# Products of the identity with itself ahead of 31 waits of TensorE, in a two-layer hybrid trunk kernel

## The chip, the cores and the metric

The kernel runs on one core of one Trainium2 chip. The metric is the device time of one execution in microseconds (us), the median of several executions. TensorE (PE in the rows) has a clock that the chip grants at one of two levels, 2.4 GHz (1.00 in the rows) and 1.2 GHz (0.50).

## What is computed

The reference is two layers of a hybrid backbone, for 128 context tokens and 256 latent tokens (384 in all, three tiles of 128) with 1024 channels, in float32. Cut to what matters here:

```
def trunk_layer(x, mod, p, ffn, is_moe, grid_pos, ctx_k, ctx_v, s0):
    shift1, scale1, gate1, shift2, scale2, gate2 = jnp.split(mod, N_MOD, axis=-1)
    h = rmsnorm(x, p['norms'][0]) * (1.0 + scale1) + shift1
    z = h @ p['w_in']
    ...
    o_a = block_attention(qa, k_all, v_all)
    o_b = chunk_gmlp(jax.nn.gelu(ub), jax.nn.gelu(vb), p['gmlp_norm'], p['gmlp_ws'], p['gmlp_bs'])
    o_c, s_fin = deltanet_mixer(qkvc, bc, ac, zc, p['dn_conv'], p['dn_a_log'], p['dn_dt_bias'], p['dn_norm'], s0)
    merged = g_a * (o_a @ wb[0]) + g_b * (o_b @ wb[1]) + g_c * (o_c @ wb[2])
    x = x + gate1 * rmsnorm(merged @ p['w_out'], p['norms'][1])
    h2 = rmsnorm(x, p['norms'][2]) * (1.0 + scale2) + shift2
    f = moe_swiglu(h2, *ffn) if is_moe else swiglu(h2, *ffn)
    x = x + gate2 * rmsnorm(f, p['norms'][3])
    return x, ka, va, s_fin

mod = (jax.nn.silu(c) @ ada_w[l] + ada_b[l])[:, None, :]
```

Layer 0 has the dense channel mixer, layer 1 the one with eight experts. The modulation vector `mod` is a product of its own, with 24 weight units of 2 MB each (12 a layer).

## The kernel before, in words

Each engine has its own program, and the engines meet through semaphores. TensorE's program is one long list that is executed strictly in its written order: a wait stops everything behind it on that engine. Weights come in units of up to 2 MB into a ring of four slots, loaded by SyncE's queue as soon as the last reader of a slot has let it go. ScalarE (ACT) rounds a unit to a high half, VectorE (DVE) or GpSimd (POOL) makes the low half, and TensorE forms each product three times (high with high, high with low, low with high). These long products (L1169 to L1171, L1205 to L1207, L1573 to L1575, L1595 to L1597, L1645 to L1647, L1707 to L1710) are most of the program.

Between them are short pieces in which TensorE takes turns with the other engines. In the order of a layer:

- `turn_x(layer, idx)` (L1142) multiplies the tokens with a diagonal of their norms, 3 token tiles by 8 channel blocks (L1152). At block 0 it waits per token tile for the diagonal of VectorE (`x_dg`), from block 4 on for the banks to be read (`h_a`, `h_d`).
- `ada_quads` and `ada_turn` (L1137, L1130) make the modulation. Their weight units (`in_ada_w`) share the ring; `ada_turn` waits for a copy by ScalarE (`ada_ev`).
- `feature_tile` (L1175): the first projections. Tile 1 waits for the low half of its weights (`p_lo`).
- The turn to attention and gating (L1295 to L1326): transposes of q and k (L1104, the line of all transposes through `tr`) after `a_ok`, then the gating products (L1319) after `tr_ev` and `v_ok`.
- Attention (L1372 to L1381): twelve steps, each with `scores` (L1341), `flip` (transposes, L1104, which wait for the exponentials, `at_e`) and `weigh` (L1362). `turn_o` transposes the outcome of a token tile after `at_n`.
- DeltaNet (from L1415): three rounds, whose gaps are filled with gate projections by `fill` (L1169 to L1171). It starts after `at_o`, and in its first round there is an `ada_turn`.
- The branch products, the output product (from L1554) with `gain_row` (L1158) ahead, then `turn_x(layer, 1)` and the channel mixer.
- At the end of layer 0 the units `n4` of the modulation (L1853) after `xk`, and then layer 1 begins with `turn_x(1, 0)`.

A product of two float32 operands is executed as two matmul instructions, so 12 such products are 24 in the trace. The order view counts products, the trace instructions.

Of the kernel before, what the change touches and what calls it, by code (L numbers as in the profile page):

```python
# [28 lines left out]
P = 128  # L29
# [5 lines left out]
NT = TOK // P  # L35
# [66 lines left out]
ADA_FIRST = (0, 1, 2, 3)  # L102
# [79 lines left out]
def build(nc, cst_d, x_prompt, x_sample, cache_k, cache_v, state_in, c, c_ctx, ada_w, ada_b, norms, w_in, qk_norm,  # L182
# [3 lines left out]
    with ctx:  # L186
# [913 lines left out]
        def _(pe):  # L1100
# [35 lines left out]

            def ada_quads(units, b):  # L1137
                for n in units:
                    for half in range(2):
                        ada_quad(n, half, b)  # L1140

            def turn_x(layer, idx, between=None, ks=range(KT)):  # L1142

                for k in ks:
                    if k == 4 and between:
                        between()
                    if k >= 4:
                        wait(pe, "h_d" if k % 2 else "h_a", layer, 4 * idx + (k - 4) // 2 + 1)
                    for t in range(NT):
                        if k == 0:  # L1150
                            wait(pe, "x_dg", layer, NT * idx + t + 1)
                        last = mm(B[T_BANK[k % 4]][:, t * P:(t + 1) * P], xt[:, t, k * P:(k + 1) * P], diag[:, t], start=True, stop=True)  # L1152
                    last.then_inc(S["xt_p"], 1)
# [21 lines left out]
            def feature_tile(layer, n):  # L1175

                bank_free(layer, n)
                wait(pe, "p_lo" if n else "v_lo", layer, lo_n(n // 4, n % 4) + 1)
                for k in range(KT):
# [35 lines left out]
            for layer in range(DEPTH):  # L1215
# [5 lines left out]
                if layer == 0:  # L1221
                    pe.wait_ge(sc_ok, 1)
                    turn_x(layer, 0, ks=range(4))
                    ada_quads(ADA_FIRST, 0)
                    ada_turn(ADA_FIRST, 0, KK_)
                    turn_x(layer, 0, ks=range(4, KT))
                    pe.wait_ge(ada_cp, set_end(ADA_FIRST))
                else:
                    turn_x(layer, 0, lambda: ada_turn(ADA_AT[0]["n4"], 7, ada_buf))

# [53 lines left out]
                for i, j0 in ((0, 8), (1, 4)):  # L1284
                    for t in range(NT):
# [7 lines left out]
                        last.then_inc(S["kvt_mm"], 1)  # L1293

                wait(pe, "a_ok", layer, 1)  # L1295
                pe.wait_ge(cache_in, 48 * (layer + 1))
# [16 lines left out]
                last.then_inc(S["tr_mm"], 1)  # L1313

                wait(pe, "tr_ev", layer, 6)
                wait(pe, "v_ok", layer, 1)
# [26 lines left out]

                def flip(i):
                    wait(pe, "at_e", layer, i + 1)
                    if i:
# [18 lines left out]

                def turn_o(t):
                    wait(pe, "at_n", layer, t + 1)
                    for j in range(4):
# [44 lines left out]

                eye2 = [eyeP.unsqueeze(1).to_broadcast([P, DNH, CHUNK])] * 2
                wait(pe, "at_o", layer, 3)  # L1415
                for pair in range(3):
# [22 lines left out]
                    if dn_ada:  # L1439
                        ada_turn(dn_ada, 0, dn_rows)  # L1440
                        pe.wait_ge(ada_cp, set_end(dn_ada))
                    fill(pair, "in")
# [86 lines left out]
                for m in range(8):  # L1529
# [8 lines left out]
                    for b in range(3):  # L1538
# [14 lines left out]
                        last.then_inc(S["br_mm"], 1)  # L1553
                ada_quads(at["wo"], 0)  # L1554
                pe.wait_ge(mod_ok, 4 * layer + 2)
                wait(pe, "br_ev", layer, 7)
                for half in range(2):
                    gain_row(layer, 2, 0, half, 2 + half)
                ada_turn(at["wo"], 0, ada_buf)
                wait(pe, "o_lo", layer, O_LO.index("me7") + 1)  # L1560
# [291 lines left out]

                if at["n4"]:  # L1853
                    wait(pe, "xk", layer, NT + 2)
                    ada_quads(at["n4"], 7)
# [1188 lines left out]
```

## Time and profile before

| | |
|---|---|
| median of 3 runs | 1894.83 us (1892.13 to 1901.94) |
| the profiled execution | 1898.18 us |
| its span, first to last instruction | 1896.4 us |
| mean granted clock over the span | 0.968 |
| TensorE busy | 1784.5 us, 94% |
| VectorE busy | 1001.0 us, 53% |
| ScalarE busy | 784.3 us, 41% |
| GpSimd busy | 257.8 us, 14% |

The profile is of one execution, 1.8 us longer than its span and 3.35 us above the median. A row of the timeline gives the start, the length, the engine and line, what is written and read, the number of instructions, and in brackets the idle time of that engine ahead of them and what ended it. A row of the windows view gives the busy time of each engine in a stretch and the clock granted in it.

### The profile page before, as it was taken

What the parts mean: (1) busy time and instruction counts of PE and PEld (TensorE: products, weight loads), DVE (VectorE), ACT (ScalarE), POOL (GpSimd) and SP (SyncE); (2) the same over time, 40 slices, a digit from 0 to 9 for tenths busy, and PEclk for the clock granted to TensorE, in tenths of its full rate; (3) what the DMA queues carried; (4) which work ended last, traced back from release to release, by engine and by line L of the source; (5) the groups of instructions that cost most, each with busy time, mean ns of one, the idle gap of its engine ahead of it and who ended that gap; (6) DMA issues with size and microseconds to landing.
All of it is one profiled execution on the core that took longest, in us unless ns stands there. A gap on an engine that the chain in (4) does not pass through costs nothing.

```text
span 1896.4 us, 31868 instructions
## 1 busy us (share of the span) xinstructions
PE 1784.5 (94%) x13834; PEld 1498.3 (79%) x13834; DVE 1001.0 (53%) x1288; ACT 784.3 (41%) x1090; POOL 257.8 (14%) x222
## 2 busy tenths in 40 slices
PE   5999899999999999998999899999999999999994
PEld 3889688888878999886989788887977555557883
DVE  2866435454644444334965345444838533446885
ACT  3354622233434222214355522234437433336774
POOL 2610032232000000002600023231002000000001
PEclk8999889999999999998999899999999999999997
DMA  9561042123644334328441052216466988979993
GB/s 354 200 223 67 30 184 95 47 91 137 218 167 134 102 121 133 133 111 287 167 171 58 8 205 68 90 47 213 173 232 223 389 295 312 352 272 392 393 376 130
DMA packets 175092, 350.75 MB, mean 185 GB/s; under 512 B 5065, under 2 KB 60385, under 8 KB 174448
## 3 DMA queue, kind: packets, MB, share of 16 engines
q1 hardware_dynamic: 171168, 335.01, 49.2%
q0 software_dynamic: 3792, 13.80, 2.1%
q8 instruction: 104, 1.70, 0.4%
q14 instruction: 28, 0.23, 0.0%
HBM read 319.43 MB, written 29.36 MB: 184 GB/s over the span
## 4 chain that ended last, share of the span: by engine, by line
PE 81%; DVE 6%; ACT 5%; DMA 5%; issue 2%; POOL 1%; SPq 0%; POOLq 0%; DVEq 0%; ACTq 0%
PE bank L1731 7%; PE bank L1169 6%; PE bank L1171 5%; PE bank L1170 5%; PE bank L1707 4%; PE bank L1710 4%; PE bank L1708 4%; PE bank L1597 3%; PE bank L1595 3%; PE bank L1596 3%; PE bank L1205 3%; PE bank L1207 3%; PE bank L1206 3%; PE bank L1410 2%; PE bank L1547 2%
## 5 line engine op out<-in xcount | busy, mean ns | idle before, releaser
L1171 PE MATMUL bank<-hT_hi,ring_split 128*128 128x384 f32 x576 | 196.7, 342 | 0.0
L1867 ACT ACTIVATE ring_split<-ring 128x1024 fp32r<-128x1024 f32 (+2 forms) x84 | 119.5, 1440 | 179.2 <-DMA ring<-in_ffn_w_up 101.1
L2746 DVE TENSOR_TENSOR ring_split<-ring,ring_split 128x2048 fp32r<-128x2048 f32 (+1 forms) x28 | 73.8, 2670 | 142.4 <-ACT ring_split L1867 142.4
L1169 PE MATMUL bank<-hT_hi,ring_split 128*128 128x384 f32 x384 | 142.9, 372 | 4.3 <-DVE modv L2417 2.9
L1207 PE MATMUL bank<-ring_split,hT_hi 128*128 128x256 f32 x480 | 137.0, 285 | 0.0
L1170 PE MATMUL bank<-hT_lo,ring_split 128*128 128x384 f32 x384 | 131.3, 342 | 0.0
L783 DVE TENSOR_TENSOR ring_split<-ring,w_upper_a 128x2048 fp32r<-128x2048 f32 (+2 forms) x54 | 96.0, 1814 | 63.5 <-PE bank L1731 39.8
L1597 PE MATMUL bank<-hT_hi,ring_split 128*128 128x384 f32 x352 | 118.8, 337 | 0.0
L1595 PE MATMUL bank<-hT_hi,ring_split 128*128 128x384 f32 x352 | 117.6, 334 | 0.0
L1596 PE MATMUL bank<-hT_lo,ring_split 128*128 128x384 f32 x352 | 117.2, 333 | 0.0
L1940 ACT ACTIVATE gates<-bank 128x384 f32<-128x384 f32 (+1 forms) x60 | 30.7, 512 | 198.8 <-PE bank L1171 164.4
L1171 PEld LDWEIGHTS bank<-hT_hi,ring_split 128*128 128x128 f32 x576 | 110.9, 193 | 0.0
L1205 PE MATMUL bank<-w_gran,hT_hi 128*128 128x256 f32 x384 | 109.1, 284 | 1.3 <-ACT ktok L1867 1.3
L1206 PE MATMUL bank<-w_gran,hT_lo 128*128 128x256 f32 x384 | 109.8, 286 | 0.0
L2491 DVE SCALAR_TENSOR_TENSOR conv<-gates,rowsT,conv 128x388 f32<-128x388 f32 x96 | 104.9, 1093 | 3.4
L778 ACT ACTIVATE w_upper_a<-ring 128x2048 fp32r<-128x2048 f32 (+2 forms) x54 | 80.4, 1529 | 55.9 <-PE bank L1710 33.2
L1731 PE MATMUL bank<-ring,hT 128*64 128x512 f32 (+1 forms) x452 | 101.4, 571 | 0.0
L1867 ACT ACTIVATE work<-bank 128x256 f32<-128x256 f32 (+1 forms) x103 | 41.1, 448 | 136.5 <-PE bank L1410 71.7
L783 DVE TENSOR_TENSOR ring_split<-ring,w_upper_b 128x2048 fp32r<-128x2048 f32 (+2 forms) x48 | 85.1, 1796 | 19.3 <-ACT w_upper_b L778 13.4
L1207 PEld LDWEIGHTS bank<-ring_split,hT_hi 128*128 128x128 f32 x480 | 92.2, 192 | 0.0
L1708 PE MATMUL bank<-ring_split,xg_hi 128*128 128x512 f32 (+1 forms) x240 | 88.8, 370 | 0.0
L778 ACT ACTIVATE w_upper_b<-ring 128x2048 fp32r<-128x2048 f32 (+2 forms) x48 | 71.4, 1516 | 34.5 <-PE bank L1710 26.7
(429 smaller groups left out, 4371.0 us busy)
## 6 DMA issues: line engine op xcount, KB each, us to landing
ring<-in_w_in SPq DMA_DIRECT2D x28, 2048.0 KB, 8.9
ring<-in_ada_w SPq DMA_DIRECT2D x24, 2048.0 KB, 12.8
ring<-in_moe_w_down SPq DMA_DIRECT2D x18, 1536.0 KB, 7.5
ring<-in_moe_w_gate SPq DMA_DIRECT2D x26, 1024.0 KB, 7.7
ring<-in_moe_w_up SPq DMA_DIRECT2D x26, 1024.0 KB, 10.0
ring<-in_w_branch SPq DMA_DIRECT2D x8, 1536.0 KB, 12.4
ring<-in_ffn_w_gate SPq DMA_DIRECT2D x11, 1024.0 KB, 5.2
ring<-in_ffn_w_up SPq DMA_DIRECT2D x11, 1024.0 KB, 7.8
```

The costliest lines, as they stand in the source:

```text
L783: op.tensor_tensor(m_half(m_place(j, visit_of(i), True), j, h), m_half(m_place(j, visit_of(i)), j, h), m_half(w_upper[j % 2], j, h).bitcas ...
L1169: mm(out, hi, hT_hi[:, k], start=k == 0, stop=False)
L1170: mm(out, hi, hT_lo[:, k], start=False, stop=False)
L1171: last = mm(out, lo, hT_hi[:, k], start=False, stop=k == KT - 1)
L1205: mm(out, hT_hi[:, k, ts], hi[k], start=k == 0, stop=False)
L1206: mm(out, hT_lo[:, k, ts], hi[k], start=False, stop=False)
L1207: last = mm(out, hT_hi[:, k, ts], lo[:, k], start=False, stop=k == KT - 1)
L1595: mm(out, w_hi(k), x_hi[:, k], start=k == 0, stop=False)
L1596: mm(out, w_hi(k), x_lo[:, k], start=False, stop=False)
L1597: last = mm(out, w_lo(k), x_hi[:, k], start=False, stop=k == n - 1)
L1708: mm(out, x_hi[:, k], lo[:, q, g], start=False, stop=False)
L1731: last = mm(out[CH[y], :, 0:w], x[:, kt], part, start=kt == 0, stop=kt == n_k - 1)
```

## The change

A helper `keep_warm(b, n, t)` issues `n` products of the 128 by 128 identity (`ident`, in the tile `cst`) with itself into 128 columns of bank `b`. Nobody reads the outcome, and no semaphore is counted up. It is called ahead of 31 waits of TensorE, with 139 products in all:

| place | wait behind it | products |
|---|---|---|
| first `ada_quads`, units 2 and 3 | arrival of the unit | 4, 12 |
| first `ada_turn`, and behind it | `ada_ev`; `h_a` | 2, 5 |
| `feature_tile` 1, layer 0 | `p_lo` | 6 |
| ahead of the transposes of q and k, layer 0 | `a_ok` | 5 |
| ahead of the gating products, both layers | `tr_ev`, `v_ok` | 8, 8 |
| `flip` 0, both layers | `at_e` | 4, 4 |
| `flip` 1 to 4, both layers | `at_e`, `at_pt` | 8 times 1 |
| last `turn_o`, both layers | `at_n` | 3, 3 |
| start of DeltaNet, both layers | `at_o` | 2, 2 |
| behind `ada_turn` in the first round, both layers | `ada_cp` | 5, 5 |
| ahead of the output product, layer 0 | `mod_ok`, `br_ev`; `ada_ev` | 4, 10 |
| third diagonal of `turn_x(0, 1)` | `x_dg` | 10 |
| units `n4` | `xk` | 10 |
| third diagonal of `turn_x(1, 0)`, and behind its `ada_turn` | `x_dg`; `h_a` | 7, 5 |
| third diagonal of `turn_x(1, 1)` | `x_dg` | 7 |

Nothing else is changed: no instruction is removed or moved against another, and no other engine's program differs.

```diff
+            def keep_warm(b, n, t=0):
+
+                for _ in range(n):
+                    mm(B[b][:, t * P:(t + 1) * P], ident, ident, start=True, stop=True)
+
+            def ada_quads(units, b, between=()):
+                for i, n in enumerate(units):
+                    if i < len(between):
+                        keep_warm(7, between[i])
                     for half in range(2):
                         ada_quad(n, half, b)
+
+            TURN_WARM = {(0, 1): 10, (1, 0): 7, (1, 1): 7}
...
                         if k == 0:
+                            if t == NT - 1:
+                                keep_warm(T_BANK[0], TURN_WARM.get((layer, idx), 0), t)
                             wait(pe, "x_dg", layer, NT * idx + t + 1)
...
                 bank_free(layer, n)
+                if layer == 0 and n == 1:
+                    keep_warm(1, 6)
                 wait(pe, "p_lo" if n else "v_lo", layer, lo_n(n // 4, n % 4) + 1)
...
-                    ada_quads(ADA_FIRST, 0)
+                    ada_quads(ADA_FIRST, 0, (0, 0, 4, 12))
+                    keep_warm(7, 2)
                     ada_turn(ADA_FIRST, 0, KK_)
+                    keep_warm(7, 5)
                     turn_x(layer, 0, ks=range(4, KT))
...
+                keep_warm(1, 8)
                 wait(pe, "tr_ev", layer, 6)
...
                 def flip(i):
+                    if i < 5:
+                        keep_warm(1, 1 if i else 4)
                     wait(pe, "at_e", layer, i + 1)
...
                 if at["n4"]:
+                    keep_warm(2, 10)
                     wait(pe, "xk", layer, NT + 2)
                     ada_quads(at["n4"], 7)
```

The other calls have the same form. L1140 is the line of the new products, and lines behind it are shifted (L1152 becomes L1163, L1319 becomes L1341, L1341 becomes L1363, L1362 becomes L1386).

TensorE's program from its start, before (L1104 transposes, L1152 `turn_x`, L1125 and L1134 the modulation, L1169 the first projection):

```order
L1104 MATMUL bank<-cst,work 128x128 x4
L1152 MATMUL bank<-diag,work 128x128 x12
L1125 MATMUL bank<-ring,small 32x512 x32
L1134 MATMUL bank<-cst,ktok 128x8 x4
L1152 MATMUL bank<-diag,work 128x128 x12
L1169 MATMUL bank<-hT_hi,w_gran 128x384
```

The same place in the changed kernel:

```order
L1104 MATMUL bank<-cst,work 128x128 x4
L1163 MATMUL bank<-diag,work 128x128 x12
L1125 MATMUL bank<-ring,small 32x512 x16
L1140 MATMUL bank<-cst 128x128 x4
L1125 MATMUL bank<-ring,small 32x512 x8
L1140 MATMUL bank<-cst 128x128 x12
L1125 MATMUL bank<-ring,small 32x512 x8
L1140 MATMUL bank<-cst 128x128 x2
L1134 MATMUL bank<-cst,ktok 128x8 x4
L1140 MATMUL bank<-cst 128x128 x5
L1163 MATMUL bank<-diag,work 128x128 x12
```

The 32 products of the modulation are now in three pieces with 4 and 12 new ones between them, and 2 and 5 stand around the turn of its outcome.

TensorE at the start of attention, before (L1319 gating products, L1104 transposes, L1341 `scores`, L1362 `weigh`):

```order
L1319 MATMUL bank<-gates,oT 128x128 x12
L1104 MATMUL bank<-cst,gates 128x128 x12
L1341 MATMUL bank<-work 128x128 x4
L1104 MATMUL bank<-cst,gates 128x128 x2
L1341 MATMUL bank<-work 128x128 x2
L1104 MATMUL bank<-cst,gates 128x128 x2
L1362 MATMUL bank<-work,gates 128x64 x2
L1341 MATMUL bank<-work 128x128 x2
```

And in the changed kernel:

```order
L1140 MATMUL bank<-cst 128x128 x8
L1341 MATMUL bank<-gates,oT 128x128 x12
L1104 MATMUL bank<-cst,gates 128x128 x12
L1363 MATMUL bank<-work 128x128 x4
L1140 MATMUL bank<-cst 128x128 x4
L1104 MATMUL bank<-cst,gates 128x128 x2
L1363 MATMUL bank<-work 128x128 x2
L1140 MATMUL bank<-cst 128x128
L1104 MATMUL bank<-cst,gates 128x128 x2
L1386 MATMUL bank<-work,gates 128x64 x2
```

Eight products stand ahead of the gating products, four ahead of the first transposes of attention, one ahead of each of the next.

TensorE at the border between the layers, in the changed kernel (before, the same rows stood without those of L1140, and those of L1163 were one piece of 12):

```order
L1140 MATMUL bank<-cst 128x128 x10
L1125 MATMUL bank<-ring,small 32x512 x16
L1163 MATMUL bank<-diag,work 128x128 x2
L1140 MATMUL bank<-cst 128x128 x7
L1163 MATMUL bank<-diag,work 128x128 x10
L1134 MATMUL bank<-cst,work 128x4 x4
L1140 MATMUL bank<-cst 128x128 x5
L1163 MATMUL bank<-diag,work 128x128 x12
```

The ten stand ahead of the units `n4`, the seven between the second and the third diagonal.

## Rows read from the trace of the kernel before

**Rows 1.** The page: the chain that ended last, by engine.

```profile
PE 81%; DVE 6%; ACT 5%; DMA 5%; issue 2%; POOL 1%; SPq 0%; POOLq 0%; DVEq 0%; ACTq 0%
```

**Rows 2.** The view of the cores: span, mean granted clock.

```profile
core 0: 1896.4 us, clock 0.968
```

**Rows 3.** Windows: stretch, length, busy (instructions) of five engines, clock, DMA share, GB/s.

```profile
31.00:45.00 14.00, 10.68 (x49) 7.46 (x49) 5.23 (x13) 5.95 (x12) 5.79 (x10) 0.51 1.05 376
...
55.00:60.00 5.00, 5.00 (x30) 5.00 (x30) 4.89 (x4) 1.50 (x3) 5.00 (x4) 1.00 0.65 240
...
244.67:249.50 4.83, 4.83 (x15) 4.83 (x16) 0.00 (x0) 0.00 (x0) 4.48 (x5) 0.50 0.72 291
...
1034.60:1038.00 3.40, 3.40 (x18) 3.40 (x17) 2.05 (x4) 3.36 (x7) 0.00 (x0) 0.50 1.05 399
1038.00:1041.40 3.40, 3.29 (x27) 2.58 (x25) 0.30 (x2) 3.40 (x9) 0.00 (x0) 1.00 0.09 31
1874.30:1896.40 22.10, 0.00 (x0) 0.00 (x0) 11.60 (x12) 7.55 (x12) 3.75 (x4) 0.50 0.56 209
```

**Rows 4.** Timeline of TensorE: products with the identity, at the full clock.

```profile
551.26 1.95 PE L1158 MATMUL bank<-cst,modv 128*128 128x128 f32 x16
```

**Rows 5.** Timeline of TensorE: the head of the kernel.

```profile
31.95 3.64 PE L1125 MATMUL bank<-ring,small 128*32 128x512 f32 x16 [3.50 <-DMA ring<-in_ada_w]
36.31 1.88 PE L1134 MATMUL bank<-cst,ktok 128*128 128x8 f32 x8 [0.72 <-ACT ktok L1867]
39.84 5.34 PE L1152 MATMUL bank<-diag,work 128*128 128x128 f32 x24 [1.65 <-ACT hT L1898]
...
51.28 0.46 PE L1169 MATMUL bank<-hT_hi,w_gran 128*128 128x384 f32 x1 [1.78 <-POOL ring_split L1007]
```

**Rows 6.** Timeline of GpSimd: its wait for the first unit of w_in.

```profile
38.92 0.92 POOL L996 DMA_DIRECT2D oT<-in_w_in  x1 [23.48 <-DMA ring<-in_w_in]
```

**Rows 7.** Timeline of TensorE, layer 0: gating, attention, start of DeltaNet.

```profile
198.42 4.52 PE L1319 MATMUL bank<-gates,oT 128*128 128x128 f32 x24 [2.27 <-ACT oT L1867]
...
207.50 0.44 PE L1104 MATMUL bank<-cst,gates 128*128 128x128 f32 x2 [1.14 <-ACT gates L2055]
...
208.56 0.65 PE L1104 MATMUL bank<-cst,gates 128*128 128x128 f32 x2 [0.20 <-ACT gates L1867]
...
219.70 0.85 PE L1104 MATMUL bank<-cst,gates 128*128 128x128 f32 x6
...
242.87 1.12 PE L1104 MATMUL bank<-cst,work 128*128 128x128 f32 x4 [1.02 <-DVE work L2590]
...
259.61 0.56 PE L1169 MATMUL bank<-hT_hi,ring_split 128*128 128x384 f32 x1 [1.45 <-DVE modv L2417]
```

**Rows 8.** Timeline of TensorE, layer 1: attention.

```profile
1053.39 0.41 PE L1104 MATMUL bank<-cst,gates 128*128 128x128 f32 x2 [0.20 <-ACT gates L1867]
...
1054.91 0.51 PE L1104 MATMUL bank<-cst,gates 128*128 128x128 f32 x2 [0.30 <-ACT gates L1867]
...
1063.82 0.85 PE L1104 MATMUL bank<-cst,gates 128*128 128x128 f32 x6 [0.48 <-ACT gates L1867]
```

**Rows 9.** Timeline of TensorE: ahead of the output product, and turn_x(0, 1).

```profile
535.96 1.63 PE L1134 MATMUL bank<-cst,work 128*128 128x4 f32 x8 [2.72 <-ACT work L1867]
...
582.66 6.81 PE L1152 MATMUL bank<-diag,work 128*128 128x128 f32 x44 [3.10 <-DVE diag L2437]
```

**Rows 10.** Timeline of TensorE: border of the layers, and turn_x(1, 1).

```profile
871.64 6.57 PE L1125 MATMUL bank<-ring,small 128*32 128x512 f32 x32 [2.87 <-DVE work L2431]
...
880.82 4.13 PE L1152 MATMUL bank<-diag,work 128*128 128x128 f32 x20 [1.97 <-DVE diag L2437]
...
887.37 4.65 PE L1152 MATMUL bank<-diag,work 128*128 128x128 f32 x24 [1.63 <-ACT hT L1898]
...
897.70 0.41 PE L1169 MATMUL bank<-hT_hi,w_gran 128*128 128x384 f32 x1 [1.53 <-ACT gates L1867]
...
1415.77 6.81 PE L1152 MATMUL bank<-diag,work 128*128 128x128 f32 x44 [2.12 <-DVE diag L2437]
```

More of the change, by code:

```diff
@@ L1135, in ada_turn @@
                 last.then_inc(ada_t, 1)
-            def ada_quads(units, b):
-                for n in units:
+            def keep_warm(b, n, t=0):
[5 more added lines that the diff above has]
+                        keep_warm(7, between[i])
                     for half in range(2):
                         ada_quad(n, half, b)
+            TURN_WARM = {(0, 1): 10, (1, 0): 7, (1, 1): 7}
             def turn_x(layer, idx, between=None, ks=range(KT)):
@@ L1228, in _, with n4_turn @@
                 else:
-                    turn_x(layer, 0, lambda: ada_turn(ADA_AT[0]["n4"], 7, ada_buf))
+                    def n4_turn():
+                        ada_turn(ADA_AT[0]["n4"], 7, ada_buf)
+                        keep_warm(1, 5)
+                    turn_x(layer, 0, n4_turn)
                 for n in range(12):
@@ L1293, in _ @@
                         last.then_inc(S["kvt_mm"], 1)
+                if layer == 0:
+                    keep_warm(1, 5)
                 wait(pe, "a_ok", layer, 1)
@@ L1366, in turn_o @@
                 def turn_o(t):
+                    if t == NT - 1:
+                        keep_warm(2, 3)
                     wait(pe, "at_n", layer, t + 1)
@@ L1414, in _ @@
                 eye2 = [eyeP.unsqueeze(1).to_broadcast([P, DNH, CHUNK])] * 2
+                keep_warm(2, 2)
                 wait(pe, "at_o", layer, 3)
@@ L1440, in _ @@
                         ada_turn(dn_ada, 0, dn_rows)
+                        keep_warm(7, 5)
                         pe.wait_ge(ada_cp, set_end(dn_ada))
@@ L1554, in _ @@
                 ada_quads(at["wo"], 0)
+                if layer == 0:
+                    keep_warm(1, 4)
                 pe.wait_ge(mod_ok, 4 * layer + 2)
@@ L1558, in _ @@
                     gain_row(layer, 2, 0, half, 2 + half)
+                if layer == 0:
+                    keep_warm(1, 10)
                 ada_turn(at["wo"], 0, ada_buf)
```

## The prediction

> **What bounds the kernel now.** I began with the chain that ended last: 81% of it is TensorE, 6% VectorE, 5% ScalarE and 5% DMA [rows 1]. So TensorE's speed is worth time nearly everywhere, also that of its clock. The mean granted clock is 0.968 over 1896.4 us [rows 2]; with two levels, 1.00 and 0.50, that is (1 - 0.968) x 1896.4 / 0.5 = 121 us at the low level. The last 22.1 us of it hold no product at all [rows 3] and cost nothing. 99 us are left, in some 18 pieces.
>
> What such a piece costs is in two windows of the same products: at the low level 15 in 4.83 us, 0.322 each, at the full one 30 in 5.00 us with the two at the bounds cut, 0.17 each [rows 3]. While TensorE runs without a pause, 46% of a low stretch is lost. 99 us would be 45 us at most, less what TensorE spends waiting there.
>
> Next, what TensorE did before the clock fell. Read the timeline rows with a bracket and ask which matmuls behind it run at half speed. 24 gating matmuls take 4.52 us behind a wait of 2.27 us [rows 7], 20 of `turn_x` take 4.13 behind 1.97, 32 of the modulation 6.57 behind 2.87 [rows 10]. The low stretches stand behind waits of 1 to 3.5 us or behind a cluster of them: each piece of low clock is the echo of a wait that is itself unavoidable for TensorE. What the change fills is those waits.
>
> **What a product costs.** The nearest row is the same form, a 128 by 128 weight with the identity as moving operand: 16 instructions, 8 products, in 1.95 us at the full clock [rows 4]. The tail of the last one is in it: a lone matmul takes 0.41 from start to end [rows 10], while its like are issued 0.17 apart [rows 3], so 0.24 is tail, and (1.95 - 0.24) / 16 = 0.11 is an instruction, 0.22 us a product. At the low level `turn_x` has 24 instructions in 5.34 us [rows 5], so (5.34 - 0.24) / 24 = 0.21 each, 0.43 a product. 139 products are 139 x 0.22 = 31 us of new work on TensorE. It costs nothing where the wait behind it is longer. The fills against the waits: 12 x 0.22 = 2.7 of 3.50; 2, 0.45 of 0.72; 5, 1.1 of 1.65; 6, 1.3 of 1.78 [rows 5]; 8, 1.8 of 2.27; 4, 0.9 of 1.14; 3, 0.67 of 1.02; 5, 1.1 of 1.45 [rows 7]; 10, 2.2 of 2.72 and of 3.10 [rows 9]; 10, 2.2 of 2.87; 7, 1.6 of 1.97 and of 2.12; 5, 1.1 of 1.63 [rows 10]. Each is 0.2 us or more inside its wait, if the clock is full while it runs. The releaser in each bracket is another engine or a DMA, whose work the fill does not touch. The exceptions are the eight single ones in attention, with waits of 0.20 and 0.30 or none [rows 7, 8]: 8 x 0.22 = 1.8 us, half of it hidden, 0.9. If every fill ran at 0.43, it would overrun nearly everywhere (10 would be 4.3 us against 2.87); that is a rival below.
>
> **What each wait gives back.** I take a term only where the slow matmuls are ahead of the next release, and cut it where another engine is next.
>
> 1. Head: 14 us are at the low level [rows 3]. The fourth modulation unit's 16 matmuls take 3.64 us [rows 5] and would take 1.9, the turn 1.88 and would take 0.95: 2.7 us. But the first unit of `w_in`, which ScalarE rounds next, lands only at 38.9 [rows 6], while that rounding starts at 40.7 now, so 1.7 of it count; the transposes behind lie beside ScalarE's work. 1.7.
> 2. `feature_tile` 1 behind 1.78 us [rows 5]: eleven matmuls at 0.32 instead of 0.17, 1.5.
> 3. Gating: of 4.52 us for 24 matmuls [rows 7] VectorE waits for the first eight, then needs about 1.1 us a tile itself: 1.5, in layer 1 1.4.
> 4. Attention, `flip` 1 to `flip` 5: 208.56 to 219.70, 11.1 us, at the low level; the same in layer 1, with part at the full one, 1053.39 to 1063.82, 10.4 us [rows 7, 8]. A step at the full clock is 1054.91 - 1053.39 = 1.5 us [rows 8]; the last steps have the wider scores and wait for ScalarE, so I estimate 1.5 + 1.6 + 3.0 + 2.3 = 8.4. Between nothing (if ScalarE sets the pace) and 5: I take 2.5, and 1.8 in layer 1.
> 5. Start of DeltaNet: four transposes take 1.12 instead of 0.66 [rows 7], and 15 products at 0.322 [rows 3] lose 15 x 0.15 = 2.2: 2.6. In layer 1 a shorter stretch, 1.5.
> 6. First `ada_turn` in DeltaNet, products from 259.61 [rows 7]: 1.6, in layer 1 1.5.
> 7. Output product behind 2.72 us: the turn 1.63 instead of 0.95 [rows 9], and 13 matmuls of 512 columns at 0.43 instead of 0.23: 3.1.
> 8. `turn_x(0, 1)`: 44 matmuls in 6.81 us [rows 9] against 44 x 0.11 + 0.24 = 5.1; cut to one stretch, 1.6. The same in layer 1 [rows 10]: 1.6.
> 9. Border of the layers: 6.57 us for 32 matmuls [rows 10] that take 3.64 at the full clock (the same count as the 16 plus 16 of the head at 1.9 each): 2.9. ScalarE and VectorE wait for their outcome before the next diagonal, so it counts. The 20 behind it: 4.13 instead of 2.5, 1.6. The 24 of 4.65 us: nothing, since TensorE waits for ScalarE at 897.70 anyway [rows 10].
>
> The sum: 1.7 + 1.5 + 2.9 + 4.3 + 4.1 + 3.1 + 3.1 + 3.2 + 4.5 = 28.4 us. Off it go 0.9 for the single fills and 0.8 for one stretch that may be new: at 897.70 TensorE waits 1.53 us without a fill [rows 10] and would wait up to 1.6 longer once the 24 ahead are fast, and the clock may fall where now it holds (half of 1.5). 26.7 us, from 1898.18 to 1871.5. The profiled execution was 3.35 above the median, so about **1868 us**.
>
> **A rule that speaks against it.** In layer 1 TensorE did almost nothing but transposes from 1034.6 to 1038.0 at the low level, and the clock then was full from 1038.0 on [rows 3]: transposes kept TensorE as busy, for the clock, as products. The Trainium skill, "TensorE: Matmul & The Clock Gate", section "Part 4: PE-mode transpose", says that a transpose does not count as activity for the clock. By that rule, the trace disagrees; were it so, the fills around transposes would be too few, which is the third rival.
>
> **The rivals.**
>
> *The idle time moves.* TensorE gets to other waits earlier, where nothing is filled (the row sums of the short convolution, tile 1 of layer 1, `a_ok` of layer 1), waits longer and the clock falls there. For it: the stretches depend on clusters of waits, not on one, and terms 3 to 5 assume that one fill mends a whole cluster. Against: most of what follows is long unbroken products. Five new stretches at 1.5: gain 19, 1876 us. 15%.
>
> *Another engine takes over.* In attention and gating ScalarE and VectorE are released by TensorE but have their own work (waits of 0.48 and 2.27). Terms 3 and 4 then shrink to a third: gain 22, 1873; inside the forecast's own range.
>
> *The transposes are not activity.* Then terms 3 to 5, whose waits stand between transposes, fail, and the single fills stay as cost: gain 28.4 - 11.3 - 1.7 = 15, 1879 us. The windows at 1034.6 and 1038.0 [rows 3] speak against it. 10%.
>
> *It does not hold the clock at all*, since the products write one place and read one operand, or since what lowers the clock is not the idle time. Fills at 0.22 are still hidden: cost 2, 1897 us. Against: products with the same identity at the full clock are in the trace and the clock held [rows 4]. 7%.
>
> *Slower.* TensorE is strictly in order, so a fill that has begun delays the real product. If the clock has fallen by the time the fills run, each takes 0.43: 10 are 4.3 against 2.87 and 3.10, 8 are 3.4 against 2.27, 12 are 5.2 against 3.50 [rows 5, 7, 9, 10]. Over all places that overruns the waits by 20 us, and with no stretch saved the kernel is at 1915 us. It decides from the point at which half the fills run at the low level without bringing the clock back (overrun 10 us). In the rows the fills begin right behind long runs at full clock, so the level is full when they start. 4%.
>
> **How the numbers follow.** The forecast, 1862 to 1874, has 64%; the rivals 15, 10, 7 and 4. A measurement of this kernel can tell about 0.5%, 9.5 us, from no change. Faster by more than that: forecast, moved idle time and transposes, 0.88 with a little taken off for what I do not see, 0.86; same 0.09; slower 0.05. The range reaches from 1860 (the sum's upper ends in terms 1 and 4) to 1884, past both partial rivals.
>
> **What would show it.** In the new profile the mean granted clock should be near 0.985, with about 22 us of low clock behind the last product and 15 to 35 ahead of it. The 32 matmuls of the modulation at the border should take 3.6 us, not 6.6; 24 gating matmuls 2.9; the 44 of `turn_x` 5.1 in both layers; the 15 products behind 244.67 0.17 each. Behind each group of L1140 a short wait should be left: where it is gone, the fill overran. `flip` 1 to `flip` 5 should take 8 to 9 us; if still 10 or more with a full clock, ScalarE sets it. The prediction is wrong if the low stretches stay behind filled waits, or if they go and the span stays.

## The result and the profile after

The changed kernel takes 1880.80 us (median of 6 runs, 1875.95 to 1885.49), the kernel before 1893.86 (6 runs, 1890.42 to 1901.94). The ratio is 0.9935, with a 95% interval of 0.9916 to 0.9955: 13 us faster, 0.7%. The forecast was 1868 us, a gain of 26.7. The sign is right and the time inside the range of 1860 to 1884, but it lies above the 1862 to 1874 that the forecast proper had, and the gain is half of what the sum gave. A second comparison of the same two kernels gave 0.9928 (0.9901 to 0.9954).

The profiled execution took 1882.91 us, 15.3 below the one of before. Its cores view [answers rows 2]:

```profile
core 0: 1881.0 us, clock 0.985
```

That is the clock that was forecast: (1 - 0.985) x 1881 / 0.5 = 56 us at the low level. Stretch by stretch it is 22.9 us behind the last product and 34.1 ahead of it, where before there were 99. The page's chain [rows 1] has now

```profile
PE 80%; DMA 7%; DVE 5%; ACT 5%; issue 2%; POOL 1%; SPq 0%; POOLq 0%; DVEq 0%; ACTq 0%
```

A little of TensorE's share has gone to DMA. The head, in the windows view (stretch, length, busy and instructions of PE, PEld, DVE, ACT, POOL, clock, DMA share, GB/s) [rows 3]:

```profile
31.00:45.00 14.00, 10.57 (x79) 8.18 (x78) 6.62 (x16) 7.30 (x16) 5.93 (x11) 1.00 1.05 375
```

14 us that were at the low level are at the full one. The timeline of TensorE there [rows 5]:

```profile
28.65 2.94 PE L1140 MATMUL bank<-cst 128*128 128x128 f32 x24
33.11 1.92 PE L1125 MATMUL bank<-ring,small 128*32 128x512 f32 x16 [1.51 <-DMA ring<-in_ada_w]
34.96 0.71 PE L1140 MATMUL bank<-cst 128*128 128x128 f32 x4
35.75 1.06 PE L1134 MATMUL bank<-cst,ktok 128*128 128x8 f32 x8
36.66 1.36 PE L1140 MATMUL bank<-cst 128*128 128x128 f32 x10
...
49.90 0.45 PE L1180 MATMUL bank<-hT_hi,w_gran 128*128 128x384 f32 x1 [0.46 <-POOL ring_split L1007]
```

Twelve new products are 24 instructions in 2.94 us, (2.94 - 0.24) / 24 = 0.11 each, as estimated. The unit's 16 matmuls take 1.92 instead of 3.64 us. The same pattern at gating and attention in layer 0 [rows 7]:

```profile
193.75 1.95 PE L1140 MATMUL bank<-cst 128*128 128x128 f32 x16
195.53 2.85 PE L1341 MATMUL bank<-gates,oT 128*128 128x128 f32 x24
...
204.20 0.38 PE L1104 MATMUL bank<-cst,gates 128*128 128x128 f32 x2
...
212.78 0.85 PE L1104 MATMUL bank<-cst,gates 128*128 128x128 f32 x6 [0.69 <-ACT gates L1900]
```

and at the output product, `turn_x(0, 1)`, the border of the layers and `turn_x(1, 1)` [rows 9, 10]:

```profile
526.89 1.05 PE L1134 MATMUL bank<-cst,work 128*128 128x4 f32 x8 [0.49 <-ACT work L1900]
...
571.70 5.18 PE L1163 MATMUL bank<-diag,work 128*128 128x128 f32 x44 [1.06 <-DVE diag L2470]
...
859.18 1.92 PE L1125 MATMUL bank<-ring,small 128*32 128x512 f32 x16 [0.64 <-DVE work L2464]
862.75 1.92 PE L1125 MATMUL bank<-ring,small 128*32 128x512 f32 x16 [1.64 <-DMA ring<-in_ada_w]
...
867.27 2.50 PE L1163 MATMUL bank<-diag,work 128*128 128x128 f32 x20 [0.40 <-DVE diag L2470]
...
1395.62 5.18 PE L1163 MATMUL bank<-diag,work 128*128 128x128 f32 x44 [0.56 <-DVE diag L2470]
```

Not one filled wait has a low stretch behind it any more: 24 gating matmuls in 2.85, 44 of `turn_x` in 5.18 twice, the modulation's in 1.92 and 1.92, 20 in 2.50. The 32 of the border still take 5.5 us from start to end instead of the 3.6 that the prediction asked for, because 1.64 us of waiting for a DMA now lie between their halves.

Most fills leave a short wait behind them, as they should. One of the larger ones does not: at `a_ok` in layer 0 TensorE comes late, behind a low stretch that is new, and its fill holds the engine until 191.1, while ScalarE's copy for it began at 189.45. In the kernel before the transposes started 0.7 us after that copy began (193.15 and 192.43), so here they stood some 1 us behind the fill. The next wait took that up: the saving is 2.9 us at 195.53, where it was 2.8 at 54.73.

Most of what is low ahead of the last product stands elsewhere. Three waits without a fill, in the timeline, and the clock around them, in the windows:

```profile
1270.40 0.36 PE L1218 MATMUL bank<-ring_split,hT_hi 128*128 128x256 f32 x1 [1.93 <-issue]
...
1410.67 7.25 PE L1718 MATMUL bank<-gates,hT 128*128 128x128 f32 x48 [1.78 <-ACT hT L1900]
...
1459.48 0.76 PE L1739 MATMUL bank<-w_upper_b,ehid_hi 128*128 128x512 f32 x1 [3.70 <-DVE ring_split L783]
```

```profile
437.50:441.50 4.00, 3.50 (x17) 3.53 (x18) 2.15 (x2) 2.95 (x3) 0.00 (x0) 0.59 1.05 402
1018.00:1024.00 6.00, 6.00 (x40) 5.67 (x40) 2.83 (x8) 5.94 (x13) 0.00 (x0) 0.72 0.83 316
1271.00:1275.50 4.50, 4.50 (x27) 4.50 (x27) 3.16 (x3) 3.69 (x4) 0.00 (x0) 0.62 1.05 393
1411.00:1415.50 4.50, 4.50 (x28) 4.50 (x27) 4.09 (x17) 3.21 (x5) 0.00 (x0) 0.62 0.12 42
1459.00:1462.90 3.90, 3.42 (x8) 2.77 (x9) 3.90 (x6) 3.05 (x3) 0.00 (x0) 0.50 1.04 393
```

The same waits stand in the profile of before, with the clock full behind them:

```profile
1292.10 0.36 PE L1205 MATMUL bank<-ring_split,hT_hi 128*128 128x256 f32 x1 [1.93 <-issue]
1292.30 0.28 PE L1206 MATMUL bank<-ring_split,hT_lo 128*128 128x256 f32 x1
...
1480.10 0.47 PE L1707 MATMUL bank<-w_upper_b,ehid_hi 128*128 128x512 f32 x1 [2.99 <-DVE ring_split L783]
```

0.28 us for a product of 256 columns is the full level (it is 0.41 at the low one), 0.47 for 512 columns too (0.76 now). The last wait grew from 2.99 to 3.70 us, the first by nothing: the clock falls behind the same 1.93 us in one execution and not in the other. The stretch at 1018 is not new: it covers the same transposes as the one from 1034.6 in the kernel before [rows 3]. It and a new one from 186 stand behind the narrow sums of the gates (4 to 16 columns), with no wait near. The stretches at 148 and 977, behind the row sums of the convolution, were there before as well (at 151 and 994), without a term in the sum.

### The profile page after: what moved, and what is told of

The parts are those of the page before. It is cut to its first block, busy times and chain, and to the rows that moved or that the text cites. A ratio compares the mean times of both kernels' runs of the same rounds, so it can differ in the third digit from the quotient of the medians.

```text
span 1881.0 us, 32424 instructions
## 1 busy us (share of the span) xinstructions
PE 1791.7 (95%) x14112; PEld 1510.1 (80%) x14112; DVE 1001.0 (53%) x1288; ACT 784.0 (42%) x1090; POOL 256.9 (14%) x222
## 4 chain that ended last, share of the span: by engine, by line
PE 80%; DMA 7%; DVE 5%; ACT 5%; issue 2%; POOL 1%; SPq 0%; POOLq 0%; DVEq 0%; ACTq 0%
PE bank L1763 6%; PE bank L1180 6%; PE bank L1182 5%; PE bank L1181 5%; PE bank L1739 4%; PE bank L1742 4%; PE bank L1740 4%; PE bank L1627 3%; PE bank L1629 3%; PE bank L1218 3%; PE bank L1628 3%; PE bank L1219 3%; PE bank L1220 3%; PE bank L1436 2%; DMA ring<-in_ada_w 2%
## 5 line engine op out<-in xcount | busy, mean ns | idle before, releaser
L1973 ACT ACTIVATE gates<-bank 128x384 f32<-128x384 f32 (+1 forms) x60 | 30.7, 512 | 191.9 <-PE bank L1182 157.5
L2524 DVE SCALAR_TENSOR_TENSOR conv<-gates,rowsT,conv 128x388 f32<-128x388 f32 x96 | 100.9, 1051 | 3.4
```

## The experiments

Executions were also read in pairs: the start of the same instruction in both, and the difference as the saving up to there. "Low clock" is the time at the low level ahead of the last product.

| kernel | median us | ratio to before, 95% | low clock in its profile |
|---|---|---|---|
| before, two profiles | 1893 to 1894 | | 99.0; 71.7 |
| the change, two profiles | 1880.80; 1879.01 | 0.9935; 0.9928 | 34.1; 20.5 |
| without the single products | 1879.47 | 0.9936 (0.9914 to 0.9958) | 27.3 |
| transposes instead of products | 1878.74 | 0.9923 (0.9895 to 0.995) | 30.7 |
| two transposes for each product | 1878.54 | 0.9924 (0.9896 to 0.9951) | 30.7 |
| every fill doubled | 1892.51 | 0.9997 (0.9975 to 1.0018) | 34.1 |
| only the fills at the long waits | 1887.12 | 0.9972 (0.9958 to 0.9986) | 75 |
| only further fills | 1888.76 | 0.9975 (0.9955 to 0.9995) | 64.9 |
| the change and the further fills | 1870.79 | 0.9878 (0.9851 to 0.9904) | 3.4 |
| the same, three fills moved or left out | 1870.54 | 0.9884 (0.9865 to 0.9904) | 3.4 |

### How much of the gain is the one profile

Both kernels again, unchanged.

> The kernel before, profiled a second time. Theory A (each unfilled wait of 1 to 3.5 us lowers the clock in some executions and not in others, by the moment at which it comes): the low stretches are partly at other places than in the first profile, among them one or more of the waits that had held the clock there (ahead of L1205 behind 447 and 1290, ahead of L1686 near 1431, ahead of L1707 near 1477), and the span is up to 8 us shorter. Theory B (the fills moved the idle time): the low stretches are at the same 18 places, with none at those four waits.

> The changed kernel again, profiled and timed. Theory A: the filled waits hold the clock again; of the unfilled ones that lowered it in the first profile (near 185, 438, 980, 1018, 1271, 1411 and 1459 us) some hold it this time and others do not; ratio 0.990 to 0.996. Theory B: the same seven places are low again.

The kernel before took 1887.29 us in this execution, with the cores row

```profile
core 0: 1885.4 us, clock 0.975
```

It has 71.7 us of low clock ahead of the last product, against 99.0 in the profile on which the forecast rests. The stretches behind tile 1, at the gating of layer 0, and at the start of DeltaNet and the `ada_turn` of layer 1 are missing; one at 1468, behind the wait for VectorE's rounding (3.77 us), is there that the first profile did not have. Missing as well is what the largest single step of the sum, the border of the layers, rests on. Its rows in this second profile of the kernel before:

```profile
864.96 1.92 PE L1125 MATMUL bank<-ring,small 128*32 128x512 f32 x16 [2.88 <-DVE work L2431]
867.35 1.92 PE L1125 MATMUL bank<-ring,small 128*32 128x512 f32 x16 [0.47 <-DMA ring<-in_ada_w]
...
871.96 2.50 PE L1152 MATMUL bank<-diag,work 128*128 128x128 f32 x20 [2.04 <-DVE diag L2437]
```

With the same waits of 2.88 and 2.04 us and no fill, the products run at the full level. The changed kernel's second profile has 20.5 us of low clock, not 34.1, and holds the full level at 186 and 438, where the first did not. So of the two expectations above it is theory A that holds, except that the span is 10.9 us shorter where it allowed 8. Between two executions of one kernel the end of the last product moves by 10.9 us with 27.3 us of low clock for the kernel before, and by 4.7 with 13.6 for the changed one: 0.40 and 0.35 us for each us of low clock. A straight line through the 58 timed executions of the kernel before (1884 to 1904 us, clock 0.967 to 0.980) also gives 0.35. So the length of the list of low stretches is itself a matter of the execution, by about 10 us of time. The last product of the second pair is 10.9 us earlier, of the first 17.0.

### Is it the idle time that moved: more fills, and these alone

The fills go to the waits where the changed kernel's profile shows low clock or that are like them, 54 products:

```diff
-                if layer == 0 and n == 1:
+                if n == 1:
                     keep_warm(1, 6)
...
+                    if j == 3:
+                        keep_warm(1, 3)
                     if j >= 3:
                         wait(pe, "qkn", layer, j - 1)
...
+                keep_warm(1, 7)
                 wait(pe, "s_or", layer, 6)
...
+                keep_warm(5, 3)
                 wait(pe, "oc_ev", layer, 3)
...
+                    keep_warm(2, 3)
                     pe.wait_ge(route_ok, 1)
...
+                    keep_warm(2, 7)
                     pe.wait_ge(ht_ev, 2 * NT)
...
+                            if v == 0 and j == M_GU + 1:
+                                keep_warm(1, 12)
                             main_slot(j, i)
```

> The change, and fills at the waits that it left out: 6 at tile 1 of layer 1, 3 in the row sums of the convolution (both layers), 7 ahead of L1218 at the end of DeltaNet (both layers), 3 ahead of the branch products (both), 3 and 7 at the routing of layer 1, 12 ahead of the second down slot of the first expert. Theory A: the low time ahead of the last product falls from 34 us to 5 to 20, the mean clock to 0.989 to 0.993, the time another 4 to 8 us below the changed kernel, 1872 to 1877 us. Theory C (what is missing of the forecast is waiting for DMAs and other engines, not clock): the low time falls but the span by less than 2 us.

> The kernel before with only the further fills of fill_more (tile 1 of layer 1; row sums; ahead of the products at the end of DeltaNet; branch products; routing; second down slot), none of the 139 of the change. Theory A (an unfilled wait lowers the clock by the moment at which it comes, in the kernel before as in the changed one): these waits cost the kernel before 3 to 5 us on average, ratio 0.997 to 0.999, against 8 us that the same fills gave on top of the change. Theory B (the change moved the low clock to them): they cost the kernel before nothing, ratio 0.9995 to 1.001, time 1893 to 1896 us.

With both it takes 1870.79 us (1868.26 to 1873.39), 23.5 below before, and the cores row is

```profile
core 0: 1869.7 us, clock 0.993
```

with 3.4 us of low clock left. The wait of 3.70 us is now, in its timeline,

```profile
1447.55 2.84 PE L1140 MATMUL bank<-cst 128*128 128x128 f32 x24
1451.49 0.50 PE L1745 MATMUL bank<-w_upper_b,ehid_hi 128*128 128x512 f32 x1 [1.11 <-DVE ring_split L783]
```

The time is 1 us below the range that was expected, and the other theory (the missing part is waiting, not clock) falls. Up to the last product this execution is 27.1 us ahead of the first profiled one of before, but 16.1 ahead of the second. The further fills alone are worth 1894.06 - 1888.76 = 5.3 us; on top of the change they are worth 1879.01 - 1870.79 = 8.2, compared on the same chip. So the change alone leaves 8 us to be had.

Did the change move the low clock to these waits, or was it there by chance all along? Both, as far as the runs can tell. Alone, the further fills were to be worth 3 to 5 us if these waits cost the kernel before something too, and nothing if only the change brought the low clock there: the 5.3 us speak for the first. The difference between 8 and 5 points at a share that did move, but the interval of the 5.3 alone reaches from 1 to 9 us and holds the 8. The profiles say more. Behind the four waits near 438, 1271, 1411 and 1459 the clock was low in 1 of 8 cases in the two profiles of the kernel before, and in 7 of 8 in the two of the changed kernel. As these four were picked from its first profile, the fairer count is of the others: 3 of 4 in its second, and 12 of 16 in the four kernels that have the change's fills in another form and none at these waits.

### Are transposes activity

The same places and numbers, but each product is a transpose of the identity, which is one instruction where a product is two:

```diff
-                    mm(B[b][:, t * P:(t + 1) * P], ident, ident, start=True, stop=True)
+                    tr(B[b][:, t * P:(t + 1) * P], ident)
```

> The 139 products of the fills are transposes of the identity instead (the same operands, through tr). If a transpose counts for the clock as a product does: mean granted clock 0.983 to 0.989 and ratio 0.990 to 0.996 as with the products. If it does not, as the Trainium skill has it (TensorE: Matmul & The Clock Gate, section Part 4: PE-mode transpose): the clock falls behind the filled waits as in the kernel before, mean clock near 0.968, ratio 0.999 to 1.002.

1878.74 us, no different from the change. By the Trainium skill, "TensorE: Matmul & The Clock Gate", section "Part 4: PE-mode transpose", these fills should not have held the clock; the runs disagree. But the low clock is back behind four filled waits (at 39, 250, 527 and 575), for example in the timeline at the head:

```profile
36.64 0.74 PE L1104 MATMUL bank<-cst 128*128 128x128 f32 x5
38.43 4.88 PE L1163 MATMUL bank<-diag,work 128*128 128x128 f32 x24 [1.05 <-ACT hT L1931]
```

Five transposes are 0.74 us, and 1.05 of the wait stay empty; the 24 matmuls behind need 4.88 us. Is that the kind or the length? Two transposes for every product:

> The fills are transposes of the identity, two for each product, so that they last as long as the products (a transpose is one instruction of 0.11 us, a product two). In fill_turns, with one transpose a product, the clock still fell behind the filled waits near 39, 527 and 575 us. If that was the length, not the kind: no low clock behind a filled wait now, mean clock 0.985 to 0.990, ratio 0.990 to 0.995. If transposes count for less: low stretches behind filled waits remain.

```profile
36.87 1.29 PE L1104 MATMUL bank<-cst 128*128 128x128 f32 x10
38.66 1.60 PE L1163 MATMUL bank<-diag,work 128*128 128x128 f32 x12 [0.51 <-ACT hT L1931]
```

As long as the products they hold the clock as well: the 12 behind them take 1.60 us, and no filled wait has low clock behind it. So it is the length, as far as one profile of each can show: four filled waits with low clock behind them with the short fills, none with the long ones, and none in the profiles of products. 1878.54 us, the same again; the four stretches are too small a part of it to be seen in the medians.

### What a fill costs that is too long

```diff
-                for _ in range(n):
+                for _ in range(2 * n):
```

> Every fill of the change twice as long, 278 products. At 0.22 us each, 31 us more TensorE work; the waits left behind the fills in the changed kernel sum to about 9 us, and some of what overruns lies beside slack. Forecast: 12 to 20 us slower than the changed kernel, 1892 to 1900 us, with no low clock behind filled waits. If fills were free for another reason (say, an engine behind them is the limit), the time stays at 1878 to 1883 us.

1892.51 us, inside the forecast of 1892 to 1900 and as slow as before, though the low clock is that of the change (34.1 us), and none of it behind a filled wait. The last product is 14.4 us later than in the changed kernel. In its timeline:

```profile
30.34 5.62 PE L1140 MATMUL bank<-cst 128*128 128x128 f32 x48
35.90 1.92 PE L1125 MATMUL bank<-ring,small 128*32 128x512 f32 x16
```

The unit has arrived by 32.3 us here, and its products stand behind the fill until 35.9. So 139 products more, 31 us of TensorE, cost about 14: some 17 went into what the waits had left or lay beside other engines' work, 14 stood in front of real work. The single fills are the other small case:

```diff
-                    if i < 5:
-                        keep_warm(1, 1 if i else 4)
+                    if i == 0:
+                        keep_warm(1, 4)
```

> The change without the eight single products ahead of flips 1 to 4 of attention in both layers (131 products). They were costed at 0.9 us in all. Theory: 0.3 to 1.5 us faster than the changed kernel, 1877 to 1880 us, and the clock in attention holds without them. Rival: they hold the clock there; without them it falls in attention of one or both layers and the time is 1 to 4 us longer.

1879.47 us, as the theory had it, but also the same as with them. In its timeline `flip` 1 and `flip` 5 are

```profile
203.87 0.41 PE L1104 MATMUL bank<-cst,gates 128*128 128x128 f32 x2 [0.20 <-ACT gates L1900]
...
212.51 0.84 PE L1104 MATMUL bank<-cst,gates 128*128 128x128 f32 x6 [0.69 <-ACT gates L1900]
```

8.64 us apart, against 212.78 - 204.20 = 8.58 with them. They neither cost nor hold anything that can be measured: in this profile the clock of the attention is full without them.

### Which waits count

Only the fills at waits of 1.9 us and more stay (unit 3, both gatings, the output's `ada_turn`, three `turn_x`, `n4`):

```diff
-                if layer == 0 and n == 1:
-                    keep_warm(1, 6)
...
-                    ada_quads(ADA_FIRST, 0, (0, 0, 4, 12))
-                    keep_warm(7, 2)
+                    ada_quads(ADA_FIRST, 0, (0, 0, 0, 12))
                     ada_turn(ADA_FIRST, 0, KK_)
-                    keep_warm(7, 5)
...
-                        keep_warm(1, 5)
...
-                if layer == 0:
-                    keep_warm(1, 5)
...
-                    if i < 5:
-                        keep_warm(1, 1 if i else 4)
...
-                    if t == NT - 1:
-                        keep_warm(2, 3)
...
-                keep_warm(2, 2)
...
-                        keep_warm(7, 5)
...
-                if layer == 0:
-                    keep_warm(1, 4)
```

> The changed kernel with its products of the identity left only at the waits that last 1.9 us and more in the profile of the kernel before: 12 ahead of unit 3 of the modulation, 8 ahead of each layer's gating, 10 ahead of the first `ada_turn` of the DeltaNet stage, 10, 7 and 7 at three of the `turn_x` fills, 10 at the last norm. The fills at tile 1, the attention's singles and row sums, the output product's turns and `flip` are left out. Theory A (waits of 1.0 to 1.8 us lower the clock as well when they come close together, or one after a stretch of narrow work): the low stretches of the attention and of the start of the DeltaNet stage come back (near 198 to 260 us, 1035 to 1110 us), and about half of the change's gain of 13 to 15 us is kept: 1884 to 1889 us, ratio 0.995 to 0.9975, granted clock 0.978 to 0.982. Rival B (only the long waits lower the clock): the whole gain stays, 1878 to 1881 us, ratio 0.992 to 0.9935, clock 0.985 or above, low stretches only where they are in the changed kernel.

(One fill is misplaced in this expectation: the ten that the kernel keeps stand ahead of the output's `ada_turn`, not in the DeltaNet stage.) 1887.12 us, 6 of the 13 us: theory A. The gating fill does its work, but then the wait for the first exponentials has none:

```profile
203.45 0.69 PE L1104 MATMUL bank<-cst,gates 128*128 128x128 f32 x2 [1.14 <-ACT gates L2073]
204.07 0.80 PE L1356 MATMUL bank<-work 64*128 64x128 f32 x4
204.80 0.69 PE L1104 MATMUL bank<-cst,gates 128*128 128x128 f32 x2
```

0.69 for two transposes, where they need 0.38 to 0.44: the clock fell around a wait of 1.14 us, shortly behind others of 0.48, 0.38 and 0.69, and stayed low from 202.9 to 216.5. A cluster counts, not the longest wait alone. The last kernel is the other direction: the further fills kept, the singles left out, and two places changed.

```diff
+                keep_warm(1, 4)
                 wait(pe, "g_ok", layer, 1)
...
-                if layer == 0:
-                    keep_warm(1, 5)
+                keep_warm(1, 3)
                 wait(pe, "a_ok", layer, 1)
```

> The kernel with the further fills (1870.79 us, 23.5 below the kernel before), less the eight single products in the attention stage, and with the products of the identity moved between two waits of the row stage: 4 stand ahead of the wait for `g_ok` and 3 ahead of the one for `a_ok`, in both layers. In the profile of the further fills one stretch of low clock is left ahead of the last product, of 3.4 us from 185 us of the span on, behind the narrow products of the gates' sums at that place. Theory A (waits and narrow work without fill lower the clock; a fill pays only where a low stretch would follow): that stretch goes, worth 3.4 us times 0.35 to 0.46, about 1.4 us, and the added products cost 4 x 0.22 = 0.9 us at either place where no wait covers them: 1869 to 1872 us, ratio 0.987 to 0.9885, granted clock 0.992 to 0.995. Rival B (the single products held the clock in the attention stage once the rest of the stage was quicker): a low stretch comes back near 200 to 260 us or 1030 to 1110 us, 1873 to 1877 us. Rival C (too many fills, each now pushes a product that was already late): no low stretch, but 1873 us or more.

1870.54 us: inside the 1869 to 1872 of theory A, but no gain over 1870.79. The 24 transposes ahead of `a_ok`, which took 4.38 us in the changed kernel behind the narrow sums of the gates, take

```profile
185.52 2.82 PE L1104 MATMUL bank<-cst,conv 128*128 128x128 f32 x24
```

That is not shown to be the work of the fill of four: without any fill there they take 2.82 us in the first profile of the kernel before too (at 188.68), and of the eight profiles with the change's fills or part of them, but not this one, four have the stretch and four do not. And a stretch of 3.4 us is now at 975, as in the kernel before (994) and the changed one (977). Its timeline:

```profile
970.29 0.89 PE L1289 MATMUL bank<-gates,cst 32*128 32x388 f32 x4
971.12 0.94 PE L1140 MATMUL bank<-cst 128*128 128x128 f32 x6
971.98 2.95 PE L1289 MATMUL bank<-gates,cst 32*128 32x388 f32 x10
974.86 0.39 PE L1218 MATMUL bank<-w_gran,hT_hi 128*128 128x256 f32 x1
...
975.64 0.42 PE L1220 MATMUL bank<-ring_split,hT_hi 128*128 128x256 f32 x1
```

No wait is near: the level falls behind row sums that use 32 of the 128 rows, while TensorE is busy throughout. But the kernel with the further fills has the same rows 0.9 us later, with the same fill,

```profile
972.86 2.95 PE L1289 MATMUL bank<-gates,cst 32*128 32x388 f32 x10
```

and the clock is full behind them. Same work, another moment, another level. What the moved fills gain and lose is below what the runs can tell apart.

## Why the prediction was half right

The saving at the same instruction, before against after, in the two profiled executions:

| step | forecast | measured | saving at the place (start before, after) |
|---|---|---|---|
| 1 head | 1.7 | 1.9 | first projections, 44.80, 42.95 |
| 2 `feature_tile` 1 | 1.5 | 1.4 | 1.4 at 51.28, 49.90; 2.8 at 54.73 |
| 3 gating, layer 0 | 1.5 | 1.5 | 2.9 at 198.42, 195.53; 4.4 behind |
| 4 attention, layer 0 | 2.5 | 2.6 | `flip` 1 to 5: 11.14, now 8.58 |
| 5 start of DeltaNet | 2.6 | 2.5 | 7.1 at 242.87, 235.79; 9.6 at 249.32 |
| 6 `ada_turn` | 1.6 | 1.4 | 9.8 at 259.61, 249.85; 11.1 at 262.84 |
| 7 output product | 3.1 | 3.2 | 9.1 at 535.96, 526.89; 12.3 at 543.12 |
| 8 `turn_x(0, 1)` | 1.6 | 1.6 | 11.0 at 582.66, 571.70; 12.5 behind |
| 9 border | 4.5 | 4.7 | 12.5 at 871.64, 859.18; 15.8 behind, and 1.4 lost between |
| 3 to 6, layer 1 | 6.2 | 6.2 | 15.4 at 1034.50; 21.6 at 1105.84 |
| 8 `turn_x(1, 1)` | 1.6 | 1.5 | 20.2 at 1415.77, 1395.62; 21.6 behind |
| sum | 28.4 | 28.5 | |

**The terms hold**, one by one and in sum, and with them what they rest on: the price of a product, 0.22; the steps of the attention, 8.6 us against an estimate of 8.4; the forms at the full clock, 1.9, 2.9 and 5.1 us; and the clock of 0.985. This pair is the one with the long list of low stretches, though: see the border above. And even in it the last product came only 17.0 us earlier. The other 11.5 were given back at places that the sum did not contain:

| where | us | what |
|---|---|---|
| 438 | 1.4 | low clock behind an unfilled wait of 1.93 |
| 1271 | 1.4 | the same wait in layer 1 |
| 1411 | 1.5 | low clock behind an unfilled wait of 1.78; 1.0 comes back at the waits that follow |
| 1459 | 3.4 | low clock behind a wait of 3.70, before 2.99 |
| 46 | 0.5 | wait for VectorE's low half of the tokens |
| 534 | 1.3 | wait of 0.89 for VectorE's low half of `w_out` |
| 862.75 | 1.4 | wait of 1.64 for the DMA of the `n4` units' second half |
| elsewhere | 1.6 | several small waits |

The first four less the 1.0 are 6.7 us, the three waits 3.2. Then the tail behind the last product grew from 1896.4 - 1871.4 = 25.0 to 26.6 us: 15.4 us of span are left.

**The step that failed** is the 0.8 us for "one stretch that may be new". The sum took the low stretches of one profile as the kernel's, gave a term to those behind the waits that it fills, and let the other waits stay harmless. Those 0.8 measured 6.7. The one place that was named for it, 897.70, kept the full clock in both profiles of the changed kernel, and lost it in three of its variants (from 881 to 893 us). Beside it, three waits for data that now are late, 3.2 us, were put at nothing. At the border I wrote "ScalarE and VectorE wait for their outcome" and did not ask when the weights arrive, which the half speed of the first 16 matmuls had hidden. At the head the fourth unit is waited for until 33.11 instead of 31.95 [rows 5]. In seven profiles with a fill ahead of it it lands at 33.0 to 33.4, in two others at 32.2 and 32.3, in the three without at 31.9 to 32.3; what delays it was not tried.

The prediction's account of cause was also too narrow. It called each piece of low clock the echo of a wait. Three of the first profile's 19 pieces do not fit: the one from 1034.6 [rows 3], which it read only for its transposes, stands behind the narrow gate sums, and those at 151 and 994 behind the row sums, with one wait of 0.65 us near.

The rival *the idle time moves* came nearest: low clock behind waits without a fill, and a gain of 19, where 13 to 15 were measured. I gave it 15% because "most of what follows is long unbroken products". That was no ground, for four of the new stretches stand behind the kernel's other waits, which all were in the trace of before. Its reason, that TensorE waits longer there, fits only the wait at 1459 (2.99, now 3.70); 1.93 and 1.78 us are what they were. That the waits come at another moment is what is left, and no run tried the moment by itself.

**The rest** is the one execution. The second profile of the same kernel, 1887.29, had 27 us less of low clock, and nothing to gain in step 2, in the gating of layer 0, at the border (step 9, 4.5 us) and in most of layer 1's start of DeltaNet. The mean clock of the 58 timed executions is 0.973, which is 101 us of low clock in all, against the 121 of the profiled one: 20 us less to win, by my estimate 7 to 8 us of time at 0.35 to 0.40. The forecast knew that its execution was 3.35 us above the median, but took them off the new time and kept the gain of 26.7 whole. If they come from low clock that the fills would remove, 1871.5 was already the new time and the gain 23. A forecast needs to know which stretches are always there.

*Another engine takes over* did not happen in attention, nor did *the transposes are not activity*; that was tried both ways. *It does not hold the clock* fell with the first profile. *Slower* was tried by doubling, which adds the 31 us that fills at 0.43 would have added: the rival let them overrun the waits by 20 us, and they did by 14. The clock stayed full behind the fills, so its own condition never arose. The sum's 0.9 for the single fills can't be told from nothing: leaving them out changes nothing that can be measured.

The sign, the mechanism and the cure are settled by the kernel with the further fills: once the unfilled waits are filled as well, the gain is 23.5 us in the medians. Open are what of an execution decides behind which of two equal waits the clock falls, and how much of the 8 us that were missing the change moved there and how much would have been there in an average execution without it.

## What to carry to other kernels

Where an engine's speed depends on its being busy, price a cure by all waits that could lower the clock, not by those that did in the one profile at hand: take a second profile first, and fill the others in the same step. Here fills of 60 to 80% of a wait's length worked; one that overruns delays real work, and one that left 1.05 us of a wait of 1.65 was not enough. And behind each stretch that becomes fast, look for what lands or is rounded next, a DMA as well as an engine.

## What the runs showed of the hardware

- The same kernel had 99.0 and 71.7 us of low clock in two executions, the changed one 34.1 and 20.5. A us of it is worth 0.35 to 0.40 us of time between executions, and 0.35 over 58 executions, below the 0.46 that the rows give for unbroken work.
- Behind a wait of 1.93 us the clock was low in 7 of 12 cases in kernels with the change's fills and in none of 6 in the others (the kernel before twice, the one with the long waits' fills), with the same work ahead of it; behind waits of 2.88 and 2.04 us at the border of the layers it was low in one execution of the kernel before and full in another. Around one of 1.14 us it fell at the end of a cluster.
- The clock also fell with no wait near: behind row sums that use 32 rows (at 975) and behind gate sums of 4 to 16 columns (at 186 and 1018), and behind the same sums it held in other executions.
- Transposes of the identity hold the clock as well as products of the same length (1878.5 against 1879.0 us).
- 193 products whose result nobody reads, 42 us of work on the busiest engine at 0.22 us each, make the kernel 23.5 us faster.
